# Gate/up weights with four rows to a partition, in 4 MiB transfers for three of a pair's four halves of an expert

## Chip, cores and metric

The kernel runs on one core of a Trainium2 chip. The metric is the device time of one execution in microseconds (us): before the change the median of three runs is 1096.83 us.

## What is computed

One residual block on 256 tokens of 1024 channels, all in float32: a gated merge of sparse attention and pooling, then a mixture of experts. The change is in the second part. Every token goes to the best 4 of 32 experts:

```python
def moe_ffn(h, router_w, router_b, w_gate_up, b_gate_up, w_down, b_down):
    logits = (hf @ router_w + router_b).astype(jnp.float32)
    top_vals, top_idx = lax.top_k(logits, TOP_K)
    gates = jax.nn.softmax(top_vals, axis=-1)
    ...
        gu = xb @ w_gate_up[e] + b_gate_up[e]
        gate = jnp.minimum(gu[:, :EXPERT_DIM], SWIGLU_LIMIT)
        up = jnp.clip(gu[:, EXPERT_DIM:], -SWIGLU_LIMIT, SWIGLU_LIMIT)
        act = gate * jax.nn.sigmoid(SWIGLU_ALPHA * gate) * (up + 1.0)
        return act @ w_down[e] + b_down[e]
    ...
    x = x + moe_ffn(rms_norm(x, norm2_g[l]), ...)
```

An expert's weights are 1024 x 2048 (gate and up, 8 MiB) and 1024 x 1024 (down, 4 MiB). All 32 experts are read once, 384 MiB, if no expert has over 64 tokens.

## The kernel before

Up to some 183 us the kernel computes attention, pooling, the output projection and the router. Then come the experts, two at a time: 16 pairs, for each of which up to 64 tokens of both experts are gathered, multiplied by the gate/up weights, turned, passed through SwiGLU, multiplied by the down weights and scattered back into `x`.

**Weights.** SBUF holds ten slots of 16 KiB a partition (2 MiB each, `slot`). Eight are for gate/up units (`gu_slot`): units 0 to 3 are the quarters of an even expert's 1024 rows, 4 to 7 those of the odd one. Two are for downs (`dn_slot`), each half an expert. Each is filled by one transfer (`load_gu`, L295; `load_dn`, L298), 16 KiB to a partition: two rows of gate/up, four of down. All these transfers are issued by SP, in a fixed order; each waits for the semaphore that says that TensorE has read its slot (`gu_used`, `dn_used`), and TensorE waits for the semaphore of the slot's landing (`gu_in`, `dn_in`). The order in the loop is: four gate/up units of the next even expert, two downs, four units of the odd one, two downs. The first pairs, up to `EARLY` = 5, are written out one by one with the downs further up.

**TensorE's order.** `pair` runs for a pair: `gate_up(1)`, the odd expert's gate/up with eight steps of k (two to a unit, L1448), and between them the scatter of the pair before (L1409), the turn of the gates (L1433) and ahead of the last step the gather for the pair after (L1392); then `down(0)`, half by half (L1475), with the turn of the gate/up result between the halves (L1464); then `gate_up(0)` of the next even expert, with scatters behind k = 1 and k = 3; then `down(1)`. The first pair is written out, pairs 2 to 15 are a hardware loop, the sixteenth is written out: it adds `x` into PSUM (L1483) in place of the gather, leaves out `gate_up(0)`, and the last expert's down (L1502) reads its weights from gate/up slots 0 and 1.

**Tokens.** ACT writes the normed tokens `xn` (L508). The gather takes from them, for step k, 128 columns of which every second belongs to k (`c0:c0 + 2 * P - 1:2`), because a partition of a unit holds two neighbouring rows of weights. The gathered tokens are multiplied by the norm's gain `g2`, which POOL brings in four small transfers in the same order (L397). The gather for the first pair is in three pieces (L1327, L1335), at the end of the first part, and TensorE's first use of half of slot 0 (`first_used`, L350) starts the refill.

```python
            def gates_a(expert, used, first=0, end=4):
                for i in range(first, end):
                    sp.wait_ge(gu_used[i], used)
                    load_gu(i, expert)
```

## Time and profile before

| | |
|---|---|
| median of three runs | 1096.83 us (1096.62 to 1097.91) |
| profiled execution, its own time | 1099.42 us |
| its span in the trace | 1097.0 us |
| TensorE matmuls busy | 1049.7 us, 96% |
| VectorE, ScalarE, GpSimd busy | 34%, 11%, 1% |
| transfers of SP's queue (q1) | 39568 packets, 428.11 MB, 93.3% of 16 engines' span |
| mean rate over the span | 392 GB/s |
| gate/up transfers | 127 of 2 MiB and two halves, median 29.4 us from issue to landing |
| down transfers | 63 of 2 MiB and two halves, median 22.8 us |

Busy shares are means over parts of the program that differ. The slices show in which stretch TensorE and the DMA engines are busy; the rows in order of time show, in brackets, how long an engine sat idle before an instruction and what ended that. "PE" is TensorE with its matmuls, "PEld" its weight loads, each float32 product counted as two matmuls. A start is in us from the span's start.

### The profile page before, as it was taken

The page shows a single profiled execution, that of the slowest core. Times are in us where ns is not written, and L with a number is a line of the kernel's source. Part 1 is how long each engine was busy: PE and PEld are TensorE (multiplying, and loading weights), DVE is VectorE, ACT ScalarE, POOL GpSimd, SP SyncE. Part 2 cuts the span into 40 slices and gives each one's busy share as a digit, 9 for nine tenths or more (in the row PEclk, how much of TensorE's full clock was granted, in tenths as well). Part 3 has the DMA queues.
Part 4 walks back from the last instruction along what each step waited for, and adds up shares of the span by engine and source line. Part 5 has one row for each costly group of instructions (what it writes and reads, how often), then busy time and mean ns, then how long its engine had stood idle before and what let it go on. Part 6 is the DMA issues. An engine that isn't in the chain of part 4 may idle for free.

```text
span 1097.0 us, 12185 instructions
## 1 busy us (share of the span) xinstructions
PE 1049.7 (96%) x4814; PEld 424.5 (39%) x4814; DVE 372.0 (34%) x690; ACT 118.1 (11%) x212; POOL 8.2 (1%) x17
## 2 busy tenths in 40 slices
PE   9999999999999999999999989898989899999998
PEld 6445445333433434343433324242424243323322
DVE  3797465122222222323322322222222222222322
ACT  3115102100000000000000000000000000000001
POOL 2000000000000000000000000000000000000000
PEclk9999999999999999999999999999999999999999
DMA  9905794999999999999999999999999999999996
GB/s 329 366 32 192 284 374 171 405 422 419 428 427 428 430 429 427 429 427 430 429 429 427 430 427 430 429 429 427 429 428 430 429 428 427 429 428 429 429 427 272
DMA packets 40560, 430.32 MB, mean 392 GB/s; under 512 B 4048, under 2 KB 6224, under 8 KB 15712
## 3 DMA queue, kind: packets, MB, share of 16 engines
q1 hardware_dynamic: 39568, 428.11, 93.3%
q0 software_dynamic: 688, 1.91, 0.5%
q8 instruction: 11, 0.18, 0.1%
q10 hardware_dynamic: 288, 0.08, 0.0%
q14 instruction: 5, 0.04, 0.0%
HBM read 429.03 MB, written 1.05 MB: 392 GB/s over the span
## 4 chain that ended last, share of the span: by engine, by line
PE 63%; DMA 34%; SPq 1%; issue 1%; DVE 1%; ACT 0%; DVEq 0%
DMA slot<-w_gate_up_dram 33%; PE bank L1448 21%; PE bank L1475 14%; PE bank L1392 5%; PE bank L1242 4%; PE bank L1095 4%; PE bank L1119 3%; PE bank L1464 2%; PE bank L1409 2%; PE bank L1348 2%; SPq L295 1%; PE bank L1062 1%; PE bank L1502 1%; DMA slot<-w_in_dram 1%; PE bank L1433 0%
## 5 line engine op out<-in xcount | busy, mean ns | idle before, releaser
L1448 PE MATMUL bank<-slot,scr 128*64 128x512 f32 x2048 | 469.9, 598 | 24.5 <-DMA slot<-w_gate_up_dram 24.5
L1448 PEld LDWEIGHTS bank<-slot,scr 128*64 128x64 f32 x2048 | 136.0, 136 | 322.9 <-issue 257.9
L1475 PE MATMUL bank<-slot,scr 128*64 128x512 f32 x992 | 225.4, 596 | 11.8 <-DMA slot<-w_down_dram 11.1
L1004 DVE TENSOR_TENSOR x<-bank,x 128x512 f32<-128x512 f32 x120 | 77.3, 686 | 233.5 <-PE bank L1409 233.5
L1475 PEld LDWEIGHTS bank<-slot,scr 128*64 128x64 f32 x992 | 67.6, 137 | 142.9 <-issue 118.5
L979 DVE COPY scr<-bank 128x512 f32<-128x512 f32 x32 | 22.1, 691 | 287.7 <-PE bank L1448 287.7
L985 DVE TENSOR_TENSOR scr<-bank,bgu 128x512 f32<-128x512 f32 x64 | 41.2, 686 | 106.6 <-PE bank L1464 106.6
L1409 PE MATMUL bank<-scr 64*128 64x512 f32 x240 | 67.8, 641 | 0.0
L1392 PEld LDWEIGHTS bank<-scr,xn 128*128 128x128 f32 x480 | 57.7, 196 | 12.2 <-issue 12.2
L521 ACT ACTIVATE scr<-bank 128x512 f32<-128x512 f32 x32 | 19.1, 597 | 398.7 <-PE bank L1448 398.7
L1392 PE MATMUL bank<-scr,xn 128*128 128x128 f32 x480 | 60.5, 285 | 0.0
L1095 PE MATMUL bank<-slot,scr 128*128 128x290 f32 (+1 forms) x128 | 43.8, 501 | 1.0 <-DMA slot<-w_in_dram 1.0
L1464 PEld LDWEIGHTS bank<-consts,scr 128*128 128x128 f32 x256 | 33.4, 210 | 26.9 <-issue 26.9
L1464 PE MATMUL bank<-consts,scr 128*128 128x128 f32 x256 | 39.4, 297 | 0.9 <-ACT scr L521 0.9
L525 ACT ACTIVATE scr<-scr 128x512 f32<-128x512 f32 x32 | 20.2, 631 | 184.0 <-DVE scr L989 184.0
L1409 PEld LDWEIGHTS bank<-scr 64*128 64x128 f32 x240 | 18.1, 184 | 48.6 <-issue 48.6
L1095 PEld LDWEIGHTS bank<-slot,scr 128*128 128x128 f32 x128 | 24.0, 190 | 19.8 <-issue 15.3
L533 ACT ACTIVATE scr<-bank 128x512 f32<-128x512 f32 x16 | 9.6, 597 | 189.7 <-PE bank L1433 189.7
L1119 PE MATMUL bank<-slot 128*128 128x512 f32 x64 | 28.7, 595 | 0.0
L1242 PE MATMUL bank<-slot 128*128 128x512 f32 x56 | 26.4, 600 | 0.0
L529 ACT ACTIVATE scr<-bank 128x512 f32<-128x512 f32 x31 | 18.5, 597 | 45.3 <-PE bank L1475 45.3
L993 DVE SCALAR_TENSOR_TENSOR scr<-scr 128x512 f32<-128x512 f32 x32 | 22.2, 693 | 3.3
(209 smaller groups left out, 505.7 us busy)
## 6 DMA issues: line engine op xcount, KB each, us to landing
slot<-w_gate_up_dram SPq DMA_DIRECT2D x127, 2048.0 KB, 29.4
slot<-w_down_dram SPq DMA_DIRECT2D x63, 2048.0 KB, 22.8
slot<-w_in_dram SPq DMA_DIRECT2D x12, 1024.0 KB, 15.0
slot<-w_out_dram SPq DMA_DIRECT2D x4, 1024.0 KB, 7.3
slot<-w_in_dram SPq DMA_DIRECT2D x4, 580.0 KB, 8.4
slot<-w_branch_pool_dram SPq DMA_DIRECT2D x2, 1024.0 KB, 7.4
slot<-w_branch_attn_dram SPq DMA_DIRECT2D x2, 1024.0 KB, 6.1
slot<-w_gate_up_dram SPq DMA_DIRECT2D x2, 1024.0 KB, 6.1
```

Of the source, the lines that this page charges most:

```text
L979: V.tensor_copy(gu_sb[:, 512:1024], GB[1][:, :]).then_inc(gu_copied[1], 1)
L985: V.tensor_tensor(gu1[:, 4 * h:4 * h + 4, :, :], v4(TU[h][:, :], 4, 2), bias.unsqueeze(3).to_broadcast([P, 4, 2, T]), ALU.add).then_inc(re ...
L993: V.scalar_tensor_tensor(out=up1, in0=up1, scalar=1.0, in1=gu1[:, :, 0, :], op0=ALU.add, op1=ALU.mult).then_inc(prod_ready, 1)
L1004: V.tensor_tensor(x[:, b, 512 * h:512 * h + 512], XY[h][:, :], x[:, b, 512 * h:512 * h + 512], ALU.add).then_inc(read[f"Y{j}"], 1)
L1095: ins = MM(bank[PAIR[j][b]][:, 0:n], hT[:, kc, b * P:b * P + P], w[:, k, :], start=kc == 0, stop=kc == KC - 1)
L1119: ins = MM(bank[PAIR[j][h]][:, :], lhs[:, k, b * P:b * P + P], w[:, k % 2, 512 * h:512 * h + 512], start=k == 0, stop=k == nk - 1)
L1242: ins = MM(acc[:, :], lhs[:, k, :], rhs[:, k, :], start=k == 0, stop=k == 3)
L1392: ins = MM(XY[h][:, k * P:k * P + P], xn[:, b, c0:c0 + 2 * P - 1:2], selb[:, b * P:b * P + P], start=b == 0, stop=b == NB - 1)
L1409: MM(XY[h][:, :], selgT[T * h:T * h + T, SEQ * e + b * P:SEQ * e + b * P + P], dsb[T * h:T * h + T, 512 * e:512 * e + 512], start=not with ...
L1448: ins = MM(GB[h][T * g:T * g + T, :], xgT[:, k, T * e:T * e + T], gu_slot[s][:, c0:c0 + 512], start=k == 0, stop=k == KC - 1)
L1464: ins = nc.tensor.transpose(TU[h][:, k * P:k * P + P], gu_sb[:, c0:c0 + 4 * P - 3:4], ident)
L1475: ins = MM(DB[T * h:T * h + T, :], actT[e][:, c, :], v3(dn_slot[j][:, :], 4)[:, k, 512 * h:512 * h + 512], start=c == 0, stop=c == KC - 1)
```

## The change

The ten slots become one tensor, `ring`, so that two neighbouring slots are one tile of 32 KiB a partition. The gate/up units are laid so that units 0 and 1, 2 and 3, 4 and 5, 6 and 7 are neighbours. A partition now holds four neighbouring rows of a half of an expert; a single unit (`gu_src`) reads the first or the second half of each partition's 32 KiB. From the first turn of SP's loop on (the loads for the sixth pair), `tiles` waits for two units' slots and brings both in one transfer of 4 MiB, with a semaphore `big_in`, for three of the four halves; units 6 and 7 stay single. At the start three loads swap their order, so that each slot is loaded where it was. TensorE's `gate_up` waits for a tile at k = 0 and k = 4; for this its loop is cut in two, with the fifth pair written out between them. The gather reads 128 neighbouring columns; ACT writes `xn` in that order, and POOL brings `g2` in sixteen transfers.

```diff
-        slot = [sb(f"slot{s}", UW) for s in range(SLOTS)]
-        gu_slot = [slot[s] for s in (0, 1, 6, 7, 3, 9, 4, 8)]
+        ring = sb("ring", SLOTS * UW)
+        slot = [ring[:, UW * s:UW * s + UW] for s in range(SLOTS)]
+        gu_slot = [slot[s] for s in (0, 1, 6, 7, 3, 4, 8, 9)]
+        gu_tile = [ring[:, UW * s:UW * s + 2 * UW] for s in (0, 6, 3, 8)]
...
+        big_in = [sem(f"big_in{t}") for t in range(3)]
...
+        def tile_src(e, t):
+
+            return w_gu[bass.ds(e * D + t * 4 * P, 4 * P), :].rearrange("(p k) n -> p (k n)", k=4)
+
         def gu_src(e, i):
 
-            return w_gu[bass.ds(e * D + i * 2 * P, 2 * P), :].rearrange("(p k) n -> p (k n)", k=2)
+            whole = tile_src(e, i // 2)
+            return whole[:, UW * (i % 2):UW * (i % 2) + UW]
...
             sp.wait_ge(job_ready, 2 * (BJ_WB + NB))
+            load_gu(7, 1)
+            units_used(18)
             load_gu(5, 1)
-            units_used(18)
+            sp.wait_ge(job_ready, 2 * (BJ_WA + NB))
             load_gu(6, 1)
-            sp.wait_ge(job_ready, 2 * (BJ_WA + NB))
-            load_gu(7, 1)
...
+            def tiles(expert, t, used):
+                for i in range(2):
+                    sp.wait_ge(gu_used[2 * t + i], used)
+                sp.dma_start(gu_tile[t], tile_src(expert + t // 2, t % 2)).then_inc(big_in[t], 16)
...
-                gates_a(here, q)
+                tiles(here, 0, q)
+                tiles(here, 1, q)
                 downs_b(sp.snap(2 * (it % PAIRS)), q2)
-                gates_b(here, q)
+                tiles(here, 2, q)
+                gates_b(here, q, 2, 4)
                 downs_a(here, q3)
...
-            for k in range(2):
-                for m in range(2):
-                    pool_e.dma_start(g2_t[64 * m:64 * m + 64, k:KC:2],
-                                     cols_d[k:P:2, P_G2 + m:P_G2 + KC:2], allow_slow_non_contiguous=True).then_inc(g2_in, 16)
+            for k in range(4):
+                for m in range(4):
+                    pool_e.dma_start(g2_t[32 * m:32 * m + 32, k:KC:4],
+                                     cols_d[k:P:4, P_G2 + m:P_G2 + KC:4], allow_slow_non_contiguous=True).then_inc(g2_in, 16)
...
-                nc.scalar.activation(xn[:, b, :], x[:, b, :], ACT.Copy, scale=small[:, 128 + b:129 + b]).then_inc(xn_ready, 1)
+                nc.scalar.activation(xn[:, b, :].rearrange("p (h k f) -> p h k f", h=2, k=4),
+                                     x[:, b, :].rearrange("p (h f k) -> p h k f", h=2, k=4),
+                                     ACT.Copy, scale=small[:, 128 + b:129 + b]).then_inc(xn_ready, 1)
...
-                        c0 = (4 * h + k) // 2 * 2 * P + k % 2
+                        c0 = P * (4 * h + k)
                         for b in range(NB):
-                            ins = MM(XY[h][:, k * P:k * P + P], xn[:, b, c0:c0 + 2 * P - 1:2], selb[:, b * P:b * P + P],
+                            ins = MM(XY[h][:, k * P:k * P + P], xn[:, b, c0:c0 + P], selb[:, b * P:b * P + P],
                                      start=b == 0, stop=b == NB - 1)
...
-                    if k % 2 == 0:
+                    if whole and k % 4 == 0 and s < 6:
+                        pe.wait_ge(big_in[2 * e + k // 4], landed)
+                    elif k % 2 == 0 and not (whole and s < 6):
                         pe.wait_ge(gu_in[s], landed)
...
-            with pe.Fori(2, n) as it:
+            with pe.Fori(2, EARLY) as it:
                 pair(pe.snap, it, False, False)
-            pair(pe.snap, n, False, True)
+            pair(int, EARLY, False, False, whole_a=True)
+            with pe.Fori(EARLY + 1, n) as it:
+                pair(pe.snap, it, False, False, whole_b=True, whole_a=True)
+            pair(pe.snap, n, False, True, whole_b=True)
```

How instructions move, in SP's loop. A row is a line, what is issued and, in brackets, the semaphores that it waits for; `ISA` rows hold only the wait, and the transfer behind them is the issue. Two downs and the odd expert's gate/up, before:

```order
L298 ISA [waits dn_used0]
L298 DMA slot<-w_down_dram 128x4096
L298 ISA [waits dn_used1]
L298 DMA slot<-w_down_dram 128x4096
L295 ISA [waits gu_used4]
L295 DMA slot<-w_gate_up_dram 128x4096
L295 ISA [waits gu_used5]
L295 DMA slot<-w_gate_up_dram 128x4096
L295 ISA [waits gu_used6]
L295 DMA slot<-w_gate_up_dram 128x4096
L295 ISA [waits gu_used7]
L295 DMA slot<-w_gate_up_dram 128x4096
```

The same place now:

```order
L306 ISA [waits dn_used0]
L306 DMA ring<-w_down_dram 128x4096
L306 ISA [waits dn_used1]
L306 DMA ring<-w_down_dram 128x4096
L350 ISA [waits gu_used5,gu_used4]
L350 DMA ring<-w_gate_up_dram 128x8192
L303 ISA [waits gu_used6]
L303 DMA ring<-w_gate_up_dram 128x4096
L303 ISA [waits gu_used7]
L303 DMA ring<-w_gate_up_dram 128x4096
```

Two of the six transfers have become one of twice the width, which waits for both slots; the place behind the downs is the same.

In TensorE's loop, the odd expert's gate/up up to k = 4 (L1448, now L1469) with the scatters (L1409, now L1428) and the turn of the gates (L1433, now L1452). Before:

```order
L1448 MATMUL bank<-slot,scr 64x512 [waits gu_in4]
L1448 MATMUL bank<-slot,scr 64x512 x7
L1409 MATMUL bank<-scr 128x512 [waits Y2_read,Y3_read,S_read,d_copied]
L1409 MATMUL bank<-scr 128x512
L1448 MATMUL bank<-slot,scr 64x512 [waits gu_in5]
L1448 MATMUL bank<-slot,scr 64x512 x7
L1405 REGISTER_ALU
L1409 MATMUL bank<-scr 128x512 [waits Y1_read,Y0_read]
L1409 MATMUL bank<-scr 128x512
L1448 MATMUL bank<-slot,scr 64x512 [waits gu_in6]
L1448 MATMUL bank<-slot,scr 64x512 x3
```

Now, in the second loop:

```order
L1469 MATMUL bank<-ring,scr 64x512 [waits big_in2]
L1469 MATMUL bank<-ring,scr 64x512 x7
L1428 MATMUL bank<-scr 128x512 [waits Y2_read,Y3_read,S_read,d_copied]
L1428 MATMUL bank<-scr 128x512
L1469 MATMUL bank<-ring,scr 64x512 x8
L1424 REGISTER_ALU
L1428 MATMUL bank<-scr 128x512 [waits Y1_read,Y0_read]
L1428 MATMUL bank<-scr 128x512
L1469 MATMUL bank<-ring,scr 64x512 [waits gu_in6]
L1469 MATMUL bank<-ring,scr 64x512 x3
```

The wait for the second unit has gone from between the scatters; the first wait stands for both.

## Rows read from the trace of the kernel before

**Rows 1.** The page's 40 slices: TensorE's granted clock, DMA busy tenths, GB/s.

```profile
PEclk9999999999999999999999999999999999999999
DMA  9905794999999999999999999999999999999996
GB/s 329 366 32 192 284 374 171 405 422 419 428 427 428 430 429 427 429 427 430 429 429 427 430 427 430 429 429 427 429 428 430 429 428 427 429 428 429 429 427 272
```

**Rows 2.** Stretches: busy us by engine, granted clock, DMA share, GB/s.

```profile
core 0: us, PE busy (x) PEld busy (x) DVE busy (x) ACT busy (x) POOL busy (x), PEclk, DMA share, GB/s
28.00:44.00 16.00, 16.00 (x38) 7.03 (x37) 10.37 (x32) 1.37 (x2) 0.00 (x0) 1.00 1.05 387
120.00:124.00 4.00, 4.00 (x16) 1.60 (x15) 1.95 (x4) 0.05 (x1) 0.00 (x0) 1.00 1.03 442
183.69:186.50 2.81, 2.81 (x13) 2.81 (x14) 1.46 (x7) 0.00 (x0) 0.00 (x0) 0.50 0.14 58
485.80:539.30 53.50, 53.50 (x262) 20.63 (x260) 15.87 (x28) 4.25 (x7) 0.00 (x0) 1.00 1.01 429
560.00:1060.00 500.00, 464.39 (x2206) 170.97 (x2208) 136.22 (x241) 35.81 (x59) 0.00 (x0) 1.00 1.01 429
```

**Rows 3.** TensorE in order of time: the last two takings of the last unit.

```profile
start us, us, engine line op out<-in xcount [idle before <-releaser]
1008.38 1.94 PE L1448 MATMUL bank<-slot,scr 128*64 128x512 f32 x8 [0.50 <-DMA slot<-w_gate_up_dram]
...
1057.33 3.65 PE L1448 MATMUL bank<-slot,scr 128*64 128x512 f32 x16 [0.19 <-DMA slot<-w_gate_up_dram]
1060.91 1.13 PE L1409 MATMUL bank<-scr 64*128 64x512 f32 x4
1062.22 1.94 PE L1448 MATMUL bank<-slot,scr 128*64 128x512 f32 x8 [0.18 <-DMA slot<-w_gate_up_dram]
1064.09 0.33 PE L1433 MATMUL bank<-consts,scr 128*128 128x128 f32 x1
...
1064.68 1.94 PE L1448 MATMUL bank<-slot,scr 128*64 128x512 f32 x8
1067.11 1.94 PE L1448 MATMUL bank<-slot,scr 128*64 128x512 f32 x8 [0.49 <-DMA slot<-w_gate_up_dram]
...
1081.80 1.13 PE L1490 MATMUL bank<-scr 64*128 64x512 f32 x4 [0.79 <-ACT scr L529]
1082.86 7.09 PE L1502 MATMUL bank<-slot,scr 128*64 128x512 f32 x32
```

**Rows 4.** The same view: four steps of k with two scatters, without a wait.

```profile
1024.17 3.60 PE L1448 MATMUL bank<-slot,scr 128*64 128x512 f32 x16
1027.70 1.13 PE L1409 MATMUL bank<-scr 64*128 64x512 f32 x4
1028.76 3.65 PE L1448 MATMUL bank<-slot,scr 128*64 128x512 f32 x16
1032.34 1.13 PE L1409 MATMUL bank<-scr 64*128 64x512 f32 x4
1033.40 3.65 PE L1448 MATMUL bank<-slot,scr 128*64 128x512 f32 x16
```

**Rows 5.** SP's issues in order of time; TensorE's first matmul on the swapped units.

```profile
115.22 33.36 SPq L295 DMA_DIRECT2D slot<-w_gate_up_dram  x8
...
420.01 1.94 SPq L295 DMA_DIRECT2D slot<-w_gate_up_dram  x4
...
582.49 1.92 SPq L295 DMA_DIRECT2D slot<-w_gate_up_dram  x4
608.73 5.02 SPq L298 DMA_DIRECT2D slot<-w_down_dram  x2
...
205.20 3.22 PE L1448 MATMUL bank<-slot,scr 128*64 128x512 f32 x14
```

**Rows 6.** The chain of work that ended last: start us, us, what.

```profile
1026.64 40.42 DMA slot<-w_gate_up_dram
```

**Rows 7.** DMA issues from 370 to 430 us: count, KB each, median us to landing.

```profile
slot<-w_gate_up_dram SPq DMA_DIRECT2D x7, 2048.0 KB, 20.3
```

**Rows 8.** Page: instructions by engine and instruction packets; then those of 1062 to 1063 us.

```profile
PE 1049.7 (96%) x4814; PEld 424.5 (39%) x4814; DVE 372.0 (34%) x690; ACT 118.1 (11%) x212; POOL 8.2 (1%) x17
...
q8 instruction: 11, 0.18, 0.1%
...
q8 instruction: 1, 0.02, 6.7%
```

**Rows 9.** Groups: weight loads (PEld) by line and form, and the ACT copy.

```profile
L1392 PEld LDWEIGHTS bank<-scr,xn 128*128 128x128 f32 x480 | 57.7, 196 | 12.2 <-issue 12.2
...
L1335 PEld LDWEIGHTS bank<-scr,xn 128*128 128x128 f32 x16 | 3.4, 324 | 0.6 <-DVE scr L919 0.6
...
L1128 PEld LDWEIGHTS bank<-selg 128*128 128x128 f32 x8 | 2.5, 327 | 2.2 <-DVE selg L558 1.7
...
L1307 PEld LDWEIGHTS bank<-scr 128*128 128x128 f32 x32 | 4.0, 191 | 3.6 <-issue 3.5
...
L508 ACT ACTIVATE xn<-x,small 128x1024 f32<-128x1024 f32 x2 | 2.3, 1149 | 0.5 <-DVE small L573 0.5
```

**Rows 10.** ACT, TensorE and POOL in order of time, ahead of the gather.

```profile
180.65 1.15 ACT L508 ACTIVATE xn<-x,small 128x1024 f32<-128x1024 f32 x1 [0.23 <-DVE small L573]
...
183.69 3.62 PE L1335 MATMUL bank<-scr,xn 128*128 128x128 f32 x16 [0.45 <-DVE scr L919]
...
14.21 2.47 POOL L397 DMA_DIRECT2D g<-cols_dram  x4
152.30 1.03 POOL L402 DMA_DIRECT2D scr<-b_down_dram  x2 [135.62 <-PE bank L1062]
```

More of the change, by code:

```diff
@@ L1019, in pair @@
                     make_sel(after2)
-            dve.wait_ge(g2_in, 64)
+            dve.wait_ge(g2_in, 256)
             take_xgT(1)
@@ L1046, in _ @@
                 pe.sem_inc(dn_used[j], 1)
+            for t in range(3):
+                pe.sem_inc(big_in[t], 16 * EARLY)
             for j in range(4):
@@ L1325, in gather_first @@
                 for k in range(4):
-                    c0 = (4 * h + k) // 2 * 2 * P + k % 2
-                    MM(XY[h][:, k * P:k * P + P], xn[:, 0, c0:c0 + 2 * P - 1:2], selb[:, 0:P], start=k == 0, stop=False)
+                    c0 = P * (4 * h + k)
+                    MM(XY[h][:, k * P:k * P + P], xn[:, 0, c0:c0 + P], selb[:, 0:P], start=k == 0, stop=False)
             def gather_rest():
@@ L1333, in gather_rest @@
                     for k in range(4):
-                        c0 = (4 * h + k) // 2 * 2 * P + k % 2
-                        ins = MM(XY[h][:, k * P:k * P + P], xn[:, 1, c0:c0 + 2 * P - 1:2], selb[:, P:2 * P], start=False, stop=k == 3)
+                        c0 = P * (4 * h + k)
+                        ins = MM(XY[h][:, k * P:k * P + P], xn[:, 1, c0:c0 + P], selb[:, P:2 * P], start=False, stop=k == 3)
                     ins.then_inc(done[f"X{h}"], 1)
@@ L1389, in gather @@
                     for k in range(4):
-                        c0 = (4 * h + k) // 2 * 2 * P + k % 2
+                        c0 = P * (4 * h + k)
                         for b in range(NB):
-                            ins = MM(XY[h][:, k * P:k * P + P], xn[:, b, c0:c0 + 2 * P - 1:2], selb[:, b * P:b * P + P],
+                            ins = MM(XY[h][:, k * P:k * P + P], xn[:, b, c0:c0 + P], selb[:, b * P:b * P + P],
                                      start=b == 0, stop=b == NB - 1)
@@ L1434, in gates_by_slot, with gate_up @@
                 ins.then_inc(done["S"], 1)
-            def gate_up(e, landed, copied, taken, between, whole_first=False):
+            def gate_up(e, landed, copied, taken, between, whole_first=False, whole=False):
                 for h in range(2):
@@ L1504, in last_down, with pair @@
                 ins.then_inc(dn_used[1], 1)
-            def pair(count, turn_no, first, last):
+            def pair(count, turn_no, first, last, whole_b=False, whole_a=False):
                 q, q1 = count(turn_no + 0), count(turn_no + 1)
@@ L1517, in pair @@
                     between.append((6, lambda: gather(count(turn_no + 2), q3)))
-                gate_up(1, in1, q2, None, between)
+                gate_up(1, in1, q2, None, between, whole=whole_b)
                 down(0, 0, dn_a, q2, q2)
@@ L1522, in pair @@
                 if not last:
-                    gate_up(0, in2, q3, q1, [(1, lambda: scatter_a(0, q1, q3, q4, first)), (3, lambda: scatter_a(1, q1, q3, q4, first))])
+                    gate_up(0, in2, q3, q1, [(1, lambda: scatter_a(0, q1, q3, q4, first)), (3, lambda: scatter_a(1, q1, q3, q4, first))], whole=whole_a)
                 if last:
```

## The prediction

> **What bounds the kernel now.** I read the slices of the page first, then stretches of time, then TensorE in order of time at the end, then the DMA issues. The slices [rows 1] show TensorE at its full granted clock (tenths of 9 throughout) and the DMA engines at 9 tenths from the eighth slice on. The stretches [rows 2] say which of the two is the bound: from 485.8 to 539.3 us TensorE is busy for all 53.50 us of a pair, from 560 on for 464.39 of 500 us, while the DMA share is 1.01 and the rate 429 GB/s in both. So the weights stream without a pause, TensorE eats up the stock that it had, and from 560 us on it waits for weights. A pair of experts is 24 MiB in twelve transfers of 2 MiB. TensorE takes up the last gate/up unit at 1008.38 and again at 1067.11 us [rows 3]: 58.73 us for twelve, 4.894 us each (428.6 GB/s). The starts before it are alike: 1057.33, 1062.22, 1067.11, each 4.89 us apart and each behind a short idle time that a weight load from DRAM ended. The end is then a chain on TensorE that begins when the last gate/up unit lands: 1067.07 to the last product, with one 0.79 us wait for ACT. The last downs are no bound: at 4.894 us apart behind that unit (two for the expert before, then two for the last expert) the last lands at about 1067.07 + 4 x 4.894 = 1086.6, and TensorE needs its last quarter at 1082.86 + 7.09 x 3/4 = 1088.2.
>
> So two things count: when the last gate/up unit lands, and how soon after it TensorE is there.
>
> **The change, part by part.**
>
> *Fewer, longer packets.* Eleven turns of SP's loop issue three 4 MiB transfers each, 33 in place of 66. A partition's row is 32 KiB instead of 16, so per tile each of the 16 engines moves 8 packets instead of 16. What does a packet cost beyond its bytes? From 28 to 44 us the input projection's weights (rows of 2 KiB) run at 387 GB/s with the DMA share at 1.05 [rows 2]: 2048 x 16 / 387 = 84.7 ns for a packet of an engine. A 16 KiB packet takes 16384 x 16 / 428.6 = 611.7 ns. The slope is 527.0 / 14336 = 0.03676 ns a byte, and what is left per packet is 84.7 - 75.3 = 9.4 ns. 8 packets fewer are 0.075 us for a tile, 0.225 for a pair, and 33 x 0.075 = **2.5 us earlier** for the last unit. The bounds: nothing, if a row of 32 KiB is moved as two packets or a long packet costs as much more; and 5.0 us, if all of the 9.4 ns went for these bytes. I take 2.5, since the two rows span a factor of eight in size and I go on by only two. The Trainium skill ("DMA: Bandwidth & Descriptors", section on small descriptors) puts the fixed overhead at about 3 cycles of the fabric, 3.5 ns at its 850 MHz; the row says 9.4. By the page, an estimate: 33 x 8 x 3.5 ns = 0.9 us of gain, and the sum below would be 1.6 us later.
>
> *Coarser arrival.* TensorE can start an odd expert's gate/up only when both first units are there. The tile lands two units, 9.79 us, before the last one. Behind it lie the first four steps of k with two scatters: the same piece without a wait runs from 1024.17 to 1033.40 in rows 4, 9.23 us. Then k = 4, the turn of the gates and k = 5: 1062.22 to 1064.68 plus the 1.87 us of a step of k, 4.33 us [rows 3]. Together 13.56 us, against the 9.79 in which the last unit arrives. With 0.04 us from landing to start, TensorE is at the last unit 13.60 - 9.79 = 3.81 us after it landed; before it was 0.04. Nothing behind absorbs it, since from there on TensorE waits for itself and once for ACT, and the last downs land before their need: **3.77 us later**. It doesn't pile up from pair to pair: from the last unit to the end of that pair's first down are 1024.17 - 1008.38 = 15.79 us, so TensorE is free at 3.81 + 15.79 = 19.60 us behind the landing, when the next tile lands (19.5). The even expert's two tiles cost the same kind of lag, inside the pair, where the wait for the next tile (48.7 us behind the last unit) swallows it: its second tile is there at 29.2, and four steps of k (7.1 us), a down (3.5), the turn (1.2) and the other down (3.5) end at 44.5.
>
> *SP's issues.* The tiles wait for two slots each, but the four units of a batch are issued back to back behind the downs, 1.92 us for four [rows 5], so all four slots were free by then. A lag of TensorE of 2 to 4 us delays the batch as much. The queue holds it: a unit issued at 1026.64 lands 40.42 us later [rows 6]. In the period before, the batch of 582.49 closes at 584.4, and the next issue is at 608.73, 24.3 us on; with some 40 us in the queue, over 15 us of transfers are left. Cost nothing; without that cover it would be the lag, once per pair. At the first tiles (420.01 us) the four units also go out in 1.94 us [rows 5] and units take 20.3 us to land [rows 7], so nothing dries up there either. The start's three swapped loads go to the same bytes of SBUF at the same waits; they are issued by 148.6 us and used from 205 us on [rows 4, 5].
>
> *Code.* TensorE's program gets two more copies of a pair. Queue 8 brings instructions, 0.18 MB in 11 packets [rows 8], 16 KiB each. TensorE ran 4814 matmuls, 262 of them in each of the 13 repeats of a loop's body, so 1408 stand in the program, with as many weight loads: 2816 / 11 = 256 instructions a packet. A pair's 524 are two packets and a bit, two pairs four or five. One came at 1062 us, in full stream, and the units around it stayed 4.89 us apart [rows 3, 8]. As bytes they are 0.04 us each, **0.2 us** in all. If one DMA engine carried all of them and the others waited for it, it would be 5 x 0.61 = 3.1 us.
>
> *The order of the normed tokens.* The gather's weight loads read 128 columns in a row instead of every other: 196 ns now, 191 for contiguous ones [rows 9], 32 loads a gather, 0.2 us, in pairs that the DMA bounds. On the way to the first refill of a slot the granted clock was 0.50, the lower level of 1.2 GHz, from 183.69 to 186.50 us [rows 2]; the strided loads took 324 ns there, and the contiguous ones at the very start of the program, as slow, 327 [rows 9]. Nothing. The ACT copy (1149 ns [rows 9]) now reads every fourth element; no row shows such a read from ACT. Between nothing and twice as long, its end moves from 181.80 to at most 182.95, and the gather starts at 183.69 behind DVE [rows 10]. Even then it is hidden. Twelve more small DMAs of POOL at 0.62 us each are 7.5 us, ahead of a wait of 135.62 us [rows 10]. Nothing.
>
> **Sum**: +3.77 - 2.5 + 0.2 = +1.5 us on the span of 1097.0. That profiled execution took 1099.42 by its own time, 2.6 us above the median of the runs, 1096.83; the difference is put on the median: **1098.3 us**. About 0.2% (2.2 us) is what a measurement of this kernel can tell from no change, so this counts as the same.
>
> **Rivals.**
> 1. *Long rows save nothing, or little* (the mechanism: rows of 32 KiB are cut at 16, or the cost per packet grows with its length). Then +3.77 + 0.2: 1100.8 us, slower. It decides from a saving below 1.8 us on, that is under 6.8 ns a packet. For it: no row has packets over 16 KiB. Against: the steady rise from 387 to 428.6 GB/s. Chance 0.27.
> 2. *The stream itself gets slower.* Either the code packets sit on one engine (up to 2.9 us over my sum: 1101.2), or the 16 engines meet in DRAM, since rows start 32 KiB apart now, for the tiles and for every single gate/up unit, of whose steps of 32 KiB it reads one half. The tiles' 33 x 9.79 = 323 us make 3.2 us of each per cent: 1101.5 us at one per cent. Against: steady 429 GB/s wherever rows are 16 KiB, and the undelayed packet at 1062. Chance 0.13. The Trainium skill ("DMA: Bandwidth & Descriptors", row pitch at large powers of two) tells of copies that fall from 207 to 164 GB/s between pitches of 512 KiB and 2 MiB; here a row pitch goes from 16 to 32 KiB, which no run here shows.
> 3. *Long rows stream clearly faster than the fit says*, so that the lag of 3.77 us is overpaid. Faster by over 2.2 us needs 6.2 us from the tiles' 323, 1.9%, or 437 GB/s. Short stretches do show up to 442 GB/s (120 to 124 us [rows 2]), but over 20 us and more it is 429. At 442 over all tiles: 323 x (1 - 428.6/442) = 9.8 us, 1091 us; at the edge 1094.6. Chance 0.14.
>
> **How the numbers follow.** Forecast 0.46: a saving of 1.8 to 4.9 us, 1095.9 to 1099.0. Same: 0.46 and a few hundredths of rival 2's lightest cases, 0.48; slower 0.38; faster 0.14. The range goes from 1094.5 (half of rival 3 left out) to 1101.6 (rivals 1 and 2 up to one per cent).
>
> **What would show it.** Packets of queue 1 down by about 33 x 128 = 4200 plus 33 x 16. The period of the last pairs 58.5 us instead of 58.73 (58.73 would be rival 1, more rival 2, under 58.2 rival 3). TensorE's waits per pair on tiles, none at the last unit, and the stretch from the last unit's first product to the end as before. The forecast's mechanism is wrong if TensorE still waits for the last unit; the sum is wrong if the period is.

## The result: 3.3 us slower, and the profile after

| | before | changed |
|---|---|---|
| median of 16 runs | 1097.53 us (1096.45 to 1099.78) | 1100.94 us (1097.88 to 1103.97) |
| ratio to before | | 1.0030, 95% interval 1.0024 to 1.0037 |
| profiled execution, its own time | 1099.42 us | 1100.73 us |
| its span | 1097.0 us | 1098.8 us |

By the ratio it is 3.3 us (2.6 to 4.1) slower, where +1.5 had been forecast: inside the range (1094.5 to 1101.6 us), above the 0.2% that the forecast had taken for no change. The kernel before itself has a median of 1097.53 over these 16 runs, 0.7 us above the three that the forecast started from, so the forecast time of 1098.3 is missed by 2.6 us. The page of the changed kernel, its slices and queues, beside [rows 1, 8]:

```profile
PEclk9999999999999999999999999999989999999999
DMA  9905795999999999999999999999999999999994
GB/s 327 361 37 192 285 373 195 408 426 419 428 429 428 428 429 432 428 431 431 428 431 431 427 429 431 430 430 429 434 426 434 426 434 429 431 431 429 429 425 187
...
q1 hardware_dynamic: 34816, 428.11, 92.7%
...
q8 instruction: 16, 0.26, 0.1%
```

Queue 1 moves the same 428.11 MB in 34816 packets, 4752 fewer: 33 x 128 = 4224 rows joined in pairs and 33 x 16 = 528 that go with the 33 transfers saved. So a row of 32 KiB does go as one packet. Instruction packets are 16 in place of 11. The DMA engines stay at 9 tenths. Only TensorE's clock is new: one slice reads 8, and over the stretch from 540 us on it is 0.97. By stretches (columns as in [rows 2]), first one row of before at the place that matters below, then the changed kernel:

```profile
1053.00:1057.00 4.00, 4.00 (x20) 1.07 (x16) 0.00 (x0) 0.00 (x0) 0.00 (x0) 1.00 1.01 430
```

```profile
540.00:1060.00 520.00, 489.70 (x2314) 184.97 (x2312) 140.31 (x248) 38.23 (x63) 0.00 (x0) 0.97 1.00 430
1053.77:1057.00 3.23, 3.23 (x8) 0.93 (x10) 0.00 (x0) 0.00 (x0) 0.00 (x0) 0.54 1.01 431
1057.00:1060.00 3.00, 3.00 (x14) 0.83 (x10) 0.00 (x0) 0.00 (x0) 0.00 (x0) 0.92 1.01 421
```

And TensorE in order of time. The first row is eight pairs before the last, the others are the end:

```profile
585.62 5.35 PE L1469 MATMUL bank<-ring,scr 128*64 128x512 f32 x16 [3.28 <-DMA ring<-w_gate_up_dram]
...
1053.77 5.35 PE L1469 MATMUL bank<-ring,scr 128*64 128x512 f32 x16 [3.27 <-DMA ring<-w_gate_up_dram]
1059.05 1.13 PE L1428 MATMUL bank<-scr 64*128 64x512 f32 x4
1060.11 3.65 PE L1469 MATMUL bank<-ring,scr 128*64 128x512 f32 x16
1063.69 1.13 PE L1428 MATMUL bank<-scr 64*128 64x512 f32 x4
1064.75 1.94 PE L1469 MATMUL bank<-ring,scr 128*64 128x512 f32 x8
...
1067.21 3.65 PE L1469 MATMUL bank<-ring,scr 128*64 128x512 f32 x16
1070.79 1.98 PE L1504 MATMUL bank<-x,consts 128*128 128x512 f32 x4
...
1084.67 7.09 PE L1523 MATMUL bank<-ring,scr 128*64 128x512 f32 x32
1091.69 2.85 PE L1511 MATMUL bank<-scr 64*128 64x512 f32 x12
```

TensorE takes up the odd expert's tile behind a wait in both of the first two rows, eight pairs apart: (1053.77 - 585.62) / 8 = 58.52 us. That is the forecast period (58.5), against 58.73. At 1053.77 TensorE has waited 3.27 us for the last odd tile, and the 16 matmuls behind it take 5.35 us in place of 3.65 [rows 4]: the granted clock there is 0.54 of full, mostly the lower level of 1.2 GHz, in a stretch that had 1.00 before. The last unit (k = 6, in the row of 1067.21, whose second half begins at 1069.0) is taken up without any wait, and from there to the end of the last product are 25.5 us, against 25.6 before.

The two traces don't start their streams alike. The first refill of a slot and TensorE's last product, before:

```profile
189.22 0.33 SPq L350 DMA_DIRECT2D slot<-w_gate_up_dram  x1
...
1089.87 2.85 PE L1490 MATMUL bank<-scr 64*128 64x512 f32 x12
```

Here the refill was issued at

```profile
188.16 0.33 SPq L363 DMA_DIRECT2D ring<-w_gate_up_dram  x1
```

and the granted clock hadn't fallen at 183.6 us this time (below). Counted from the first refill to the end of TensorE's last product (its start plus 2.85 us), before took 903.50 us and the changed kernel 906.38: **+2.9 us**. That measure is free of the start and of the stores at the end, and I use it for all traces. Three traces of the kernel before give 903.50, 903.55 and 903.13, so it scatters by 0.4 us.

### The profile page after: what moved, and what is told of

Same layout as the page of the kernel before. It is cut to its first block, busy times and chain, and to the rows that moved or that the text cites. A ratio compares the mean times of both kernels' runs of the same rounds, so it can differ in the third digit from the quotient of the medians.

```text
span 1098.8 us, 12125 instructions
## 1 busy us (share of the span) xinstructions
PE 1053.5 (96%) x4814; PEld 426.7 (39%) x4814; DVE 372.1 (34%) x690; ACT 120.1 (11%) x212; POOL 14.2 (1%) x29
## 3 DMA queue, kind: packets, MB, share of 16 engines
q1 hardware_dynamic: 34816, 428.11, 92.7%
## 4 chain that ended last, share of the span: by engine, by line
PE 73%; DMA 25%; SPq 1%; DVE 1%; issue 0%; ACT 0%; DVEq 0%
PE bank L1469 30%; DMA ring<-w_gate_up_dram 24%; PE bank L1496 13%; PE bank L1411 5%; PE bank L1261 4%; PE bank L1114 4%; PE bank L1428 4%; PE bank L1138 3%; PE bank L1485 2%; PE bank L1367 2%; PE bank L1452 1%; PE bank L1081 1%; PE bank L1523 1%; DMA ring<-w_in_dram 1%; SPq L306 0%
## 5 line engine op out<-in xcount | busy, mean ns | idle before, releaser
L1469 PE MATMUL bank<-ring,scr 128*64 128x512 f32 x2048 | 482.1, 614 | 33.6 <-DMA ring<-w_gate_up_dram 33.3
L1469 PEld LDWEIGHTS bank<-ring,scr 128*64 128x64 f32 x2048 | 142.0, 140 | 336.8 <-issue 292.2
L1496 PE MATMUL bank<-ring,scr 128*64 128x512 f32 x992 | 225.0, 595 | 0.0
L1496 PEld LDWEIGHTS bank<-ring,scr 128*64 128x64 f32 x992 | 68.7, 137 | 127.5 <-issue 123.7
L1428 PE MATMUL bank<-scr 64*128 64x512 f32 x240 | 67.7, 641 | 0.0
L1411 PEld LDWEIGHTS bank<-scr,xn 128*128 128x128 f32 x480 | 54.7, 192 | 12.2 <-issue 12.2
L1411 PE MATMUL bank<-scr,xn 128*128 128x128 f32 x480 | 57.6, 278 | 0.0
L1114 PE MATMUL bank<-ring,scr 128*128 128x290 f32 (+1 forms) x128 | 43.8, 501 | 1.3 <-DMA ring<-w_in_dram 1.2
L1428 PEld LDWEIGHTS bank<-scr 64*128 64x128 f32 x240 | 18.1, 184 | 49.3 <-issue 49.3
L1114 PEld LDWEIGHTS bank<-ring,scr 128*128 128x128 f32 x128 | 24.0, 190 | 20.1 <-issue 15.3
L1138 PE MATMUL bank<-ring 128*128 128x512 f32 x64 | 28.7, 596 | 0.0
L1261 PE MATMUL bank<-ring 128*128 128x512 f32 x56 | 26.4, 600 | 0.0
```

The lines of the kernel that those rows point to most:

```text
L1114: ins = MM(bank[PAIR[j][b]][:, 0:n], hT[:, kc, b * P:b * P + P], w[:, k, :], start=kc == 0, stop=kc == KC - 1)
L1138: ins = MM(bank[PAIR[j][h]][:, :], lhs[:, k, b * P:b * P + P], w[:, k % 2, 512 * h:512 * h + 512], start=k == 0, stop=k == nk - 1)
L1261: ins = MM(acc[:, :], lhs[:, k, :], rhs[:, k, :], start=k == 0, stop=k == 3)
L1411: ins = MM(XY[h][:, k * P:k * P + P], xn[:, b, c0:c0 + P], selb[:, b * P:b * P + P], start=b == 0, stop=b == NB - 1)
L1428: MM(XY[h][:, :], selgT[T * h:T * h + T, SEQ * e + b * P:SEQ * e + b * P + P], dsb[T * h:T * h + T, 512 * e:512 * e + 512], start=not with ...
L1469: ins = MM(GB[h][T * g:T * g + T, :], xgT[:, k, T * e:T * e + T], gu_slot[s][:, c0:c0 + 512], start=k == 0, stop=k == KC - 1)
```

## Experiments

Each was timed beside the kernel before, but for the last two, which are that kernel again, one run each. "Behind the refill" is the measure above, from the run's trace. "Lag" is how much later than its landing TensorE takes up the last gate/up unit.

| run | median us | ratio, 95% interval | span us | behind the refill us |
|---|---|---|---|---|
| before (first trace) | 1097.53 | | 1097.0 | 903.50 |
| changed kernel | 1100.94 | 1.0030 (1.0024 to 1.0037) | 1098.8 | 906.38 |
| e1, coarse wait only | 1102.95 | 1.0058 (1.0044 to 1.0071) | 1100.1 | 908.22 |
| e2, code copies only | 1097.88 | 1.0010 (1.0001 to 1.0019) | 1096.9 | 903.56 |
| e3, seven matmuls in the wait | 1114.25 | 1.0157 (1.0144 to 1.0171) | 1112.4 | 920.41 |
| e4, last tile in units | 1095.71 | 0.9982 (0.9973 to 0.9991) | 1093.8 | 902.09 |
| e5, three matmuls in the wait | 1098.74 | 1.0012 (1.0003 to 1.0020) | 1096.5 | 904.51 |
| e6, rows of four, single units | 1097.08 | 0.9994 (0.9985 to 1.0003) | 1096.1 | 903.87 |
| e7, odd expert in units | 1096.11 | 0.9988 (0.9979 to 0.9996) | 1094.1 | 902.25 |
| e8, rows of 8 KiB | 1105.22 | 1.0069 (1.0056 to 1.0082) | 1102.5 | 911.23 |
| e9, e4 and three matmuls | 1095.15 | 0.9971 (0.9961 to 0.9982) | 1093.2 | 901.03 |
| e10, four tiles, last in units | 1094.97 | 0.9969 (0.9956 to 0.9981) | 1092.8 | 900.54 |
| e11, before again | one run, 1099.11 | | 1097.1 | 903.55 |
| e12, before a third time | one run, 1097.53 | | 1095.4 | 903.13 |

The theory when the first four were written: the packets gain 2.5 us, the coarse arrival costs 3.8, and a fall of TensorE's clock behind the one long wait costs 1.7 more.

**e1: the coarse wait alone, on the kernel before.**

```diff
-                    if k % 2 == 0:
+                    if k % 2 == 0 and s != 5:
                         pe.wait_ge(gu_in[s], landed)
+                        if s == 4:
+                            pe.wait_ge(gu_in[5], landed)
```

> The kernel before, with one edit: TensorE waits for units 4 and 5 of the odd expert together ahead of k = 0. Transfers, rows and code stay as before. Theory (the changed kernel pays for the coarse arrival and for a fall of TensorE's clock behind the one long wait): in the changed kernel's trace TensorE idles 3.27 us ahead of the tile and the 16 matmuls behind it take 5.35 us in place of 3.65, at a granted clock of 0.5. So 3.8 + 1.7 = 5.5 us at the last unit, 1.0050 of before; the wait is longer here (about 6 us, since the even expert keeps its units), so up to 7 us if the lower clock lasts longer. Rival A (coarse arrival alone, the clock costs nothing at the end): +3.8 us. Rival B (the changed kernel's loss sits in the long rows or the code): 0 to +0.5 us.

Measured: 1.0058, 6.4 us (4.8 to 7.8). TensorE's last pair and last products:

```profile
1055.08 5.28 PE L1450 MATMUL bank<-slot,scr 128*64 128x512 f32 x16 [3.29 <-DMA slot<-w_gate_up_dram]
...
1092.93 2.85 PE L1492 MATMUL bank<-scr 64*128 64x512 f32 x12
```

The wait was 3.29 us and not 6, since the lag of each pair is there when the next one begins. The second unit was in at 1055.04, so the last lands 9.79 us later, at 1064.83. The last products are 1092.93 - 1089.87 = 3.06 us later than in [rows 3]'s trace, so the last unit is taken up at 1067.11 + 3.06 = 1070.17: a lag of 5.3 us, for 3.81 + 1.7 forecast. (The second unit was in 1055.04 - 187.56 = 867.48 us behind the refill, where before has 868.07; since the transfers are the same, that is scatter of 0.6 us in the stream.) One wait, with no byte moved otherwise, costs more than the whole change does; rival B is out, and rival A (3.8) lies below the interval.

**e2: the code copies alone.**

```diff
-            with pe.Fori(2, n) as it:
+            with pe.Fori(2, EARLY) as it:
+                pair(pe.snap, it, False, False)
+            pair(int, EARLY, False, False)
+            with pe.Fori(EARLY + 1, n) as it:
                 pair(pe.snap, it, False, False)
```

> The kernel before, with TensorE's loop cut in two around a written-out fifth pair, nothing else. Theory: four or five instruction packets more, 0.04 us each, at most +0.2 us (ratio 1.0002). Rival (one DMA engine carries them and the others wait for it): up to +3.1 us, 1.003, which would by itself be the changed kernel's loss.

Measured: 1.0010, with an interval from 0.1 to 2.1 us. Its queue of instructions and TensorE's end:

```profile
q8 instruction: 16, 0.26, 0.1%
```

```profile
1062.14 1.94 PE L1448 MATMUL bank<-slot,scr 128*64 128x512 f32 x8 [0.18 <-DMA slot<-w_gate_up_dram]
...
1067.03 1.94 PE L1448 MATMUL bank<-slot,scr 128*64 128x512 f32 x8 [0.49 <-DMA slot<-w_gate_up_dram]
...
1089.79 2.85 PE L1490 MATMUL bank<-scr 64*128 64x512 f32 x12
```

Four or five packets more (the three traces of before have 11, 12 and 12), and behind the refill 903.56 us against 903.50: nothing in the trace. The stated rival (3.1 us) is out. The median allows up to 2 us that this one trace doesn't show.

**e3 and e5: TensorE kept busy in the wait, on the changed kernel.**

```diff
+                    if whole and e == 1 and k == 0:
+                        for _ in range(7):
+                            MM(GB[0][:, 0:K_W], ident, consts[:, :], start=True, stop=True)
                     if whole and k % 4 == 0 and s < 6:
```

> The changed kernel, with seven matmuls of constants (128x480, into a bank that the real product then overwrites; about 3 us) ahead of the wait for the odd expert's tile, so that TensorE is busy for most of the 3.27 us. Nothing of the output changes. Theory: the granted clock stays 1.00, the 16 matmuls behind the tile take 3.65 us again, and the end comes 1.7 us earlier than in the changed kernel: 1.6 us over before (1.0015) where the changed kernel has 3.3 (1.0030). Rival A (the clock's fall is swallowed elsewhere): as the changed kernel, 1.003. If the matmuls themselves came in the way, later than the changed kernel.

Measured: 1.0157, a miss of my own making. I had sized seven such matmuls at 3 us:

```profile
1003.90 5.90 PE L1464 MATMUL bank<-consts 128*128 128x480 f32 x14
1009.73 3.65 PE L1472 MATMUL bank<-ring,scr 128*64 128x512 f32 x16
...
1025.06 3.17 PE L1411 MATMUL bank<-scr,xn 128*128 128x128 f32 x26
```

They take 5.9 us (two passes of 0.42 us each), more than the wait. The gather of one pair is 1025.06 - 965.75 = 59.31 us behind the other's, and no wait is left:

```profile
600.00:1050.00 450.00, 450.00 (x2094) 174.24 (x2092) 120.93 (x213) 32.16 (x53) 0.00 (x0) 1.00 1.00 425
```

TensorE, busy for all of the 450 us, became the bound, and the stream followed it at 425 GB/s. With three, in e5:

> As the run with seven matmuls in the wait, but with three, which are 6 x 0.42 = 2.5 us by that run's rows (seven took 5.90 us, more than the wait, and made TensorE the bound). 0.7 to 0.8 us of idle time are left. Theory: the granted clock stays 1.00, the 16 matmuls behind the tile take 3.65 us, and the end is 1.7 us ahead of the changed kernel: about 1.6 us over before (1.0015). Rival (the clock's fall costs nothing at the end): as the changed kernel, 1.003.

Measured: 1.0012, against 1.0030. Before and behind the last odd tile:

```profile
1048.67 2.68 PE L1464 MATMUL bank<-consts 128*128 128x480 f32 x6
1053.12 3.65 PE L1472 MATMUL bank<-ring,scr 128*64 128x512 f32 x16 [1.76 <-DMA ring<-w_gate_up_dram]
```

```profile
1053.12:1057.00 3.88, 3.88 (x18) 1.36 (x20) 0.00 (x0) 0.00 (x0) 0.00 (x0) 1.00 1.01 431
```

1.76 us idle, clock 1.00, 3.65 us for the 16 matmuls, and behind the refill 904.51: 1.87 us less than the changed kernel (forecast 1.7). What's left, +1.0 us, is the lag less the packets' gain: the last unit is taken up 3.8 us behind its landing, as the prediction had it, and the tile was in 2.7 us earlier behind the refill than before. This separates the two costs: the low clock is 1.7 us of the loss by the 16 matmuls (5.35 against 3.65), 1.9 by the whole trace.

**e4: the last odd tile as two single units.** SP's loop ends one turn earlier (VectorE computes that count), and the last turn is written out.

```diff
-                tiles(here, 2, q)
-                gates_b(here, q, 2, 4)
+                if not last:
+                    tiles(here, 2, q)
+                gates_b(here, q, 0 if last else 2, 4)
...
-                    if whole and k % 4 == 0 and s < 6:
+                    if units and k % 2 == 0 and s < 6:
+                        pe.wait_ge(gu_in[s], 16 * EARLY + 16)
+                    elif whole and k % 4 == 0 and s < 6:
```

> The changed kernel, but SP's last turn brings units 4 and 5 of the last odd expert as single transfers, and TensorE waits for them one by one; 32 long transfers stay. (One small VectorE instruction more computes the count of turns for SP.) Theory: the lag at the last unit is gone but for 0.6 us that the pair before hands on, the packets' gain stays: -2.4 + 0.6 + 0.2 = -1.6 us against before, 0.9985. Rival A (the lag is the pairs' rhythm and not the last tile's): as the changed kernel, +3.3 us. Rival B (long rows save nothing): +0.8 us.

Measured: 0.9982, and 1.4 us less than before behind the refill. So the loss sits at the last tile, and the packets' gain is real.

```profile
994.21 6.57 PE L1478 MATMUL bank<-ring,scr 128*64 128x512 f32 x16 [3.50 <-DMA ring<-w_gate_up_dram]
...
1059.73 1.94 PE L1478 MATMUL bank<-ring,scr 128*64 128x512 f32 x8
...
1062.18 3.65 PE L1478 MATMUL bank<-ring,scr 128*64 128x512 f32 x16
1065.77 1.98 PE L1513 MATMUL bank<-x,consts 128*128 128x512 f32 x4
...
1086.66 2.85 PE L1520 MATMUL bank<-scr 64*128 64x512 f32 x12
```

The low clock of the pair before (6.57 us for 16 matmuls) is handed on as a lag of about 1 us, where 0.6 had been expected; then TensorE runs through with no wait at all.

**e6: the change without its long transfers.** SP's side of the edit; TensorE's loop and waits are those of before.

```diff
-                tiles(here, 0, q)
-                tiles(here, 1, q)
+                gates_a(here, q)
                 downs_b(sp.snap(2 * (it % PAIRS)), q2)
-                tiles(here, 2, q)
-                gates_b(here, q, 2, 4)
+                gates_b(here, q)
```

> The changed kernel without its long transfers: all gate/up units stay single (16 KiB rows that start 32 KiB apart), TensorE's loop and waits as before; the tokens' order, the ACT copy and POOL's sixteen small transfers as in the change. Theory: all of this is hidden, 1.000 of before (within 0.3 us), period 58.73 us. Rival (rows that start 32 KiB apart read more slowly): 3.2 us for each per cent of rate.

Measured: 0.9994 (-1.6 to +0.3 us). Its gathers are 1008.44 - 949.67 = 58.77 us apart. The order of the tokens, the ACT copy, POOL's transfers and rows at steps of 32 KiB cost nothing that these runs show. One thing in its trace stands out:

```profile
1060.43 1.94 PE L1463 MATMUL bank<-ring,scr 128*64 128x512 f32 x8 [0.19 <-DMA ring<-w_gate_up_dram]
...
1066.18 1.94 PE L1463 MATMUL bank<-ring,scr 128*64 128x512 f32 x8 [1.36 <-DMA ring<-w_gate_up_dram]
```

with, from 1062 to 1066 us,

```profile
q8 instruction: 1, 0.02, 1.7%
```

The last unit came 5.75 us behind the one before it, not 4.89: an instruction packet fell between them, and this time the unit was 0.86 us late. Whether the packet did it isn't shown. In e11 one fell between the last two units as well (one packet of queue 8 from 1060.8 to 1065.5 us), and they were 1065.60 - 1060.71 = 4.89 us apart.

**e7: only the even expert in long transfers.** SP's side of the edit; TensorE's waits follow it.

```diff
-                tiles(here, 2, q)
-                gates_b(here, q, 2, 4)
+                gates_b(here, q)
```

> The changed kernel with only the even expert's two tiles long (22 transfers of 4 MiB), the odd expert in four units. Theory: 22 x 0.075 = 1.65 us gained, the wait for an even tile costs clock only inside the pair, of which some 0.6 us reach the last unit, code +0.2: -0.9 us against before, 0.9992; period 58.58 us. Rival (any tile's wait ends in a lag at the end): over +2 us.

Measured: 0.9988, behind the refill 1.25 us less (forecast 0.9). Gathers are 1007.05 - 948.48 = 58.57 us apart (58.58).

```profile
966.11 3.65 PE L1468 MATMUL bank<-ring,scr 128*64 128x512 f32 x16 [3.75 <-DMA ring<-w_gate_up_dram]
...
1024.70 5.35 PE L1468 MATMUL bank<-ring,scr 128*64 128x512 f32 x16 [3.77 <-DMA ring<-w_gate_up_dram]
...
1066.06 1.98 PE L1503 MATMUL bank<-x,consts 128*128 128x512 f32 x4
...
1086.96 2.85 PE L1510 MATMUL bank<-scr 64*128 64x512 f32 x12
```

The clock falls here too, behind 3.77 us of waiting for the last even tile (5.35 us), and it's paid inside the pair. One pair earlier it didn't fall: 3.75 us of waiting, and the 16 matmuls took 3.65 us. So the length of the wait alone doesn't decide.

**e8: twice the packets, on the kernel before.**

```diff
-            return w_gu[bass.ds(e * D + i * 2 * P, 2 * P), :].rearrange("(p k) n -> p (k n)", k=2)
+            return w_gu[bass.ds(e * D + i * 2 * P, 2 * P), :].rearrange("(k p) n -> p k n", p=P)
```

> The kernel before with twice as many packets for the same bytes: a partition holds rows p and p + 128 of a unit, so a unit of 2 MiB goes in rows of 8 KiB; the gather reads 128 neighbouring columns, the gain comes in one transfer. Each unit has 8 packets more on an engine. Theory (9.4 ns a packet, from the two rates of the trace): 0.075 us a unit, 8 units a pair: period 58.73 + 0.60 = 59.33 us, and 120 units behind the start of the stream make +9.0 us, 1.0082. Rival (some 3.5 ns a packet, by the Trainium skill, "DMA: Bandwidth & Descriptors"; an estimate): period 58.95, +3.4 us, 1.0031.

Measured: 1.0069, 7.6 us (6.1 to 9.0), 7.7 us behind the refill.

```profile
953.67 1.94 PE L1445 MATMUL bank<-slot,scr 128*64 128x512 f32 x8 [0.57 <-DMA slot<-w_gate_up_dram]
...
1013.02 1.94 PE L1445 MATMUL bank<-slot,scr 128*64 128x512 f32 x8 [0.58 <-DMA slot<-w_gate_up_dram]
...
1095.37 2.85 PE L1487 MATMUL bank<-scr 64*128 64x512 f32 x12
```

The last unit is taken up every 1013.02 - 953.67 = 59.35 us, forecast 59.33 by 9.4 ns a packet. The Trainium skill ("DMA: Bandwidth & Descriptors", "Why small descriptors are slow (HBM only)") states a fixed overhead of about 3 cycles a packet, at its 850 MHz 3.5 ns, an estimate. That would have given 58.95, and the trace disagrees. (59.35 - 58.73) / 64 = 9.7 ns a packet; the changed kernel gives (58.73 - 58.52) / 24 = 8.8. The total is 1.3 us under 120 x 0.075 = 9.0; why isn't shown.

**e9 and e10: what would beat both kernels.** e9 is e4 with e5's three matmuls in the pairs that still have an odd tile; e10 is e4 with units 6 and 7 as a fourth tile in all turns but the last.

> The run with the last tile in units (0.9982 of before, where -1.6 us had been forecast), and with it three matmuls of constants in the wait for the other odd tiles (2.5 us of the 3.3). Theory: the clock stays at 1.00 in the last pairs, so the 0.6 us of lag that the second-last pair handed on is gone: 0.5 us faster than that run, 0.9977. Rival (the clock in the pairs before reaches the end by more than that): up to 1.7 us faster.

> The run with the last tile in units, and units 6 and 7 of the odd experts before the last as a fourth long transfer: 42 long transfers in place of 32. Theory: 10 x 0.075 = 0.75 us earlier for the last unit, period 58.73 - 4 x 0.075 = 58.43 us; but TensorE comes out of the second-last pair later by half a pair's unit, of which up to 0.6 us reach the end: between 0.0 and 0.75 us faster than the run with three tiles, 0.9975 to 0.9982. Rival (long packets on all gate/up rows save more or less than by their number): period off 58.43.

Measured: 0.9971 and 0.9969, both some 3 us faster than before, and some 6 than the changed kernel. In e9 the matmuls, then the tile:

```profile
990.76 2.68 PE L1471 MATMUL bank<-consts 128*128 128x480 f32 x6
994.96 3.65 PE L1481 MATMUL bank<-ring,scr 128*64 128x512 f32 x16 [1.52 <-DMA ring<-w_gate_up_dram]
```

The clock held, and it ends 1.06 us ahead of e4 behind the refill (forecast 0.5; e4's fall in that pair was a long one, 6.57 us for the 16 matmuls, where three of its other tiles took 5.35). In e10 the last two odd tiles and the last products:

```profile
936.15 5.17 PE L1480 MATMUL bank<-ring,scr 128*64 128x512 f32 x16 [3.18 <-DMA ring<-w_gate_up_dram]
...
994.57 4.98 PE L1480 MATMUL bank<-ring,scr 128*64 128x512 f32 x16 [3.35 <-DMA ring<-w_gate_up_dram]
...
1085.63 2.85 PE L1522 MATMUL bank<-scr 64*128 64x512 f32 x12
```

The tiles are 58.42 us apart, forecast 58.43. Behind the refill it is 1.55 us ahead of e4, twice the 0.75 at most that had been expected, and the two traces say where that comes from. The last odd tile is taken up 994.57 - 187.94 = 806.63 us behind the refill here and 994.21 - 187.42 = 806.79 in e4, and behind it neither trace has a wait for a transfer. But the 16 matmuls at that place took 4.98 us here and 6.57 in e4. So nearly all of the surplus is how long the clock was low in one execution and in the other, and not the fourth tile. The medians of e4, e9 and e10 can't be told apart: their intervals overlap.

**e11 and e12: is the early fall of the clock the program's?**

> The kernel before, once more, for its trace alone. The granted clock fell to 0.50 at 183.6 us in the trace of before, for 3.4 us, and the first refill was issued at 189.22; in the run with the coarse waits, which has the same program up to there, it stayed at 1.00 and the refill came at 187.56. If the fall is chance, this trace may show either; if it is the program's, again 0.50 and 189.2 us. The last unit should be taken up 878 us behind the first refill.

> The kernel before a third time, for the same question: how often the granted clock is 0.50 at 183.6 us. With the clock at 1.00 the span should be shorter by the 1.1 to 1.7 us by which the first refill is earlier.

Measured: the same kernel as in [rows 2], from 183.69 us on:

```profile
183.69:185.00 1.31, 1.31 (x13) 1.31 (x13) 0.88 (x5) 0.00 (x0) 0.00 (x0) 1.00 0.18 75
```

```profile
187.66 0.33 SPq L350 DMA_DIRECT2D slot<-w_gate_up_dram  x1
```

Clock 1.00, the refill 1.56 us earlier than in the first trace, and the same 903.55 us from there on. e12 has its refill at 188.04. Of the 14 traces the first of before and e2's show the fall; e1, e11 and e12 run the same gather without it. So the program doesn't fix it, and the refill is 1.2 to 1.6 us later with it; what starts the fall isn't shown. e11's span is none the less 1097.1 us, since it ends 6.1 us behind the issue of the last stores (1091.00), and before's 4.5 (1092.52).

## Why the prediction came out as it did

**Right, by the forecast's steps.** The packets' gain, 2.5 us: the last odd tile was in at 1053.73 - 188.16 = 865.57 us behind the refill, and the second of the same two units before at 1057.29 - 189.22 = 868.07. That is 2.5 us earlier, as worked out. One trace against another scatters by up to 0.6 us here (e1), and the period is the firmer evidence: 11 turns at 58.73 - 58.52 make 2.3. The 0.2 for code isn't seen (e2: 0.06). The cost of a packet, 9.4 ns from the rates at 2 and 16 KiB, held at 8 KiB (9.7) and at 32 KiB (8.8). The coarse arrival was right in its mechanism and in where it matters: TensorE doesn't wait for the last unit any more, nothing behind absorbs the lag (25.5 us to the end, against 25.6), and with the last tile in units (e4) the loss is gone. The lag of 3.8 us without the low clock is what e5 shows. The swapped loads, the tokens' order and POOL's transfers cost nothing that e6 shows, and SP's waits for two slots cost nothing that the period of 58.52 us shows.

**Where it failed: the lag was short by 1.7 us.** "*Together 13.56 us, against the 9.79 in which the last unit arrives*": the 13.56 us were taken from rows without a wait [rows 4] or behind one of 0.18 us [rows 3]. The prediction had a long wait in its own working (TensorE is done at 44.5 us and the tile lands at 48.7), and hadn't asked what the clock does behind it. TensorE idles 3.27 us, the granted clock goes to its lower level of 1.2 GHz, the first 16 matmuls take 5.35 us, and four steps of k with two scatters take 1064.75 - 1053.77 = 10.98 us, not 9.23. The lag is 5.5 us, not 3.81 (taken up at 1069.0, landed at 1053.73 + 9.79 = 1063.52). So the sum is -2.5 + 5.5 = +3.0; the trace has +2.9 behind the refill, the runs 3.3 (2.6 to 4.1). The trace of before held a hint: the clock at 0.50 from 183.69 us on [rows 2], behind short waits of TensorE, from which I took only that strided loads are no slower.

That the time lies in the range all the same is luck more than merit. The upper part of the range was there for rivals 1 and 2, and neither is what happened. By its own edge of 0.2% for a change the prediction gave "same" 0.48 and "slower" 0.38, and it came out slower.

**The rivals.** Rival 1 (long rows save nothing) would have given almost the measured time, 1100.8, and is wrong: the period is 58.52 and the packets are whole. By the time alone it would have passed for the cause. Rival 2 is out at the sizes that it named by e2 and e6, rival 3 by the period. The fall of the clock was in none of the cases.

**Left open.** How much of the 0.4 us between the runs' 3.3 and the trace's 2.9 is scatter; e2's median (0.1 to 2.1 us) beside its trace, which shows nothing; what decides whether the clock falls behind a wait, and for how long; what the fourth tile of e10 is worth by itself. The changed kernel's runs spread over 6.1 us, those of before over 3.3; that the length of the fall at the last tile makes part of this is likely, but only one of them has a trace.

## What to carry to other kernels

Where transfers bound this kernel, a longer transfer gained here only its packets' fixed part, 0.075 us for 4 MiB, and it moved work behind its own landing. Sum that up at the last transfers before the end, where nothing hides it, and leave those short: the same change with its last tile in units is 0.2% faster instead of 0.3% slower (0.3% faster with a busy TensorE, though that step lies within the scatter of the runs). When one wait takes the place of several, ask what TensorE's clock does behind it, and price the work that follows at both levels.

## What the hardware showed that I had not expected

- TensorE's granted clock fell to 0.50 behind single waits in an otherwise full pair, and the next 16 matmuls took 5.3 us in place of 3.65 (behind waits of 3.27 us in the changed kernel, 3.29 in e1, 3.77 in e7; 6.57 us in one pair of e4, behind 3.50). From 560 us on, the shortest wait with a fall was 2.33 us (e1, at 937.63 us). Behind waits of up to 1.76 us (e5), 2.19 (changed kernel, at 878.24 us) and once 3.75 (e7, at 966.11 us) the 16 matmuls took 3.65 us.
- With three matmuls of constants in the wait (2.68 us busy) the clock stayed at 1.00, and the end came 1.9 us earlier (e5).
- The same program shows the early fall at 183.6 us in one execution and not in another (e11 and e12 against the first trace); the refill comes 1.2 to 1.6 us earlier without it.
- With an instruction packet between them, the last two units came 4.89 us apart in two traces of before (the first and e11) and 5.75 in e6. No run shows that the packet caused the delay, but "it cost nothing once" was weaker evidence than the prediction made of it.
